# Row norms applied behind the projections instead of ahead of them, in a hybrid encoder layer with experts

## The reference

```python
def rms_norm(x, w):
    y = xf * lax.rsqrt(jnp.mean(xf * xf, axis=-1, keepdims=True) + NORM_EPS)
    return y * w
...
    xn = rms_norm(x, norm1_w)
    proj = xn @ w_in                                   # (tokens, 4096)
    hq, hf_f, hf_b, hi, hg, aq, ak, av = jnp.split(proj, split_points(), axis=-1)
    o_hg = hgrn2_bidirectional(hq, hf_f, hf_b, hi, hg, lb_f, lb_b, hg_norm_w)
    o_da = diff_attention(aq, ak, av, layer, q_norm_w, k_norm_w, lq1, lk1, lq2, lk2, subln_w)
    h = x + (jnp.concatenate([o_hg, o_da], axis=-1) @ w_out)
    return h + expert_choice_moe(rms_norm(h, norm2_w), router_w, w1, w3, w2)
```

## Time and profile before

| | |
|---|---|
| median of 3 runs | 2069.92 us (2067.45 to 2071.37) |
| profiled execution | 2071.38 us, of which the span of the trace is 2069.6 |
| TensorE busy | 2022.5 us, 98% of the span |
| VectorE busy | 1616.7 us, 78% |
| ScalarE busy | 1339.1 us, 65% |
| GpSimd busy | 86.3 us, 4% |
| mean granted TensorE clock | 0.990 |

### The profile page before, as it was taken

The page is one execution under the profiler, slowest core; times in us unless marked ns, Lnnn a source line. Parts: engine busy times, 40 slices in busy tenths (PEclk is TensorE's granted clock), DMA queues, the critical chain, the costliest instruction groups (busy, mean ns, idle before and its releaser), DMA issues.

```text
span 2069.6 us, 27968 instructions
## 1 busy us (share of the span) xinstructions
PE 2022.5 (98%) x10828; PEld 1556.4 (75%) x10828; DVE 1616.7 (78%) x1187; ACT 1339.1 (65%) x1027; POOL 86.3 (4%) x51
## 2 busy tenths in 40 slices
PE   7999999989799999999999999999999999999998
PEld 6899998768677777777777777777777777776776
DVE  4247766764888888888888888888888888888886
ACT  4234433742477777777777777777777777778774
POOL 0000000300000000000000000000000000000000
PEclk9999999989899999999999999999999999999999
DMA  5222224125599999999999999999999999999994
GB/s 162 67 67 74 95 76 160 64 99 195 197 370 365 394 359 390 366 381 377 372 390 363 394 355 392 363 387 373 375 383 362 394 360 399 356 389 369 376 386 152
DMA packets 192388, 618.17 MB, mean 299 GB/s; under 512 B 13680, under 2 KB 38000, under 8 KB 192336
## 3 DMA queue, kind: packets, MB, share of 16 engines
q1 hardware_dynamic: 188640, 604.86, 77.8%
q0 software_dynamic: 3696, 12.59, 2.7%
HBM read 596.96 MB, written 20.45 MB: 298 GB/s over the span
## 4 chain that ended last, share of the span: by engine, by line
PE 95%; DVE 3%; DMA 1%; ACT 1%; issue 0%; POOL 0%; SPq 0%; POOLq 0%; ACTq 0%; DVEq 0%
PE pair L582 29%; PE pair L584 29%; PE pair L583 29%; PE pair L663 2%; PE pair L938 1%; PE pair L736 1%; PE pair L760 1%; PE pair L721 1%; PE pair L884 1%; PE pair L747 0%; DMA x_in<-x 0%; DVE top_tokens L1660 0%; PE pair L703 0%; DMA v_tm<-projected 0%; PE pair L801 0%
## 5 line engine op out<-in xcount | busy, mean ns | idle before, releaser
L1743 DVE TENSOR_TENSOR chunk_low<-ring,chunk_high 128x3072 fp32r<-128x3072 f32 (+1 forms) x384 | 1182.2, 3088 | 221.1 <-ACT chunk_high L1206 221.1
L1206 ACT ACTIVATE chunk_high<-ring 128x3072 fp32r<-128x3072 f32 (+1 forms) x384 | 981.2, 2564 | 212.4 <-PE pair L584 212.1
L582 PE MATMUL pair<-chunk_high,xe_high 128*96 128x512 f32 (+1 forms) x1536 | 579.3, 377 | 1.4 <-DVE xe_low L1737 1.4
L584 PE MATMUL pair<-chunk_high,xe_low 128*96 128x512 f32 (+1 forms) x1536 | 574.8, 374 | 0.0
L583 PE MATMUL pair<-chunk_low,xe_high 128*96 128x512 f32 (+1 forms) x1536 | 573.1, 373 | 0.0
L582 PEld LDWEIGHTS pair<-chunk_high,xe_high 128*96 128x96 f32 x1536 | 248.1, 162 | 90.1 <-DVE chunk_low L1743 2.6
L584 PEld LDWEIGHTS pair<-chunk_high,xe_low 128*96 128x96 f32 x1536 | 247.8, 161 | 90.1
L583 PEld LDWEIGHTS pair<-chunk_low,xe_high 128*96 128x96 f32 x1536 | 248.4, 162 | 87.3
L582 PE MATMUL pair<-chunk_high,hid_high 128*96 128x512 f32 x704 | 280.3, 398 | 0.0
L584 PE MATMUL pair<-chunk_high,hid_low 128*96 128x512 f32 x704 | 276.9, 393 | 0.0
L583 PE MATMUL pair<-chunk_low,hid_high 128*96 128x512 f32 x704 | 276.2, 392 | 0.0
(11 more groups left out here) (209 smaller groups left out, 1855.8 us busy)
## 6 DMA issues: line engine op xcount, KB each, us to landing
ring<-w SPq DMA_DIRECT2D x288, 1536.0 KB, 9.3
ring<-w SPq DMA_DIRECT2D x96, 1024.0 KB, 8.5
raw_w<-w_in SPq DMA_DIRECT2D x16, 1024.0 KB, 5.4
projected<-stage SPq DMA_DIRECT2D x36, 128.0 KB, 1.7
wo_raw<-w_out SPq DMA_DIRECT2D x8, 512.0 KB, 3.4
x_in<-x SPq DMA_DIRECT2D x6, 512.0 KB, 7.8
queries_and_keys<-qk_raw SPq DMA_DIRECT2D x8, 384.0 KB, 2.8
x_again<-x SPq DMA_DIRECT2D x6, 512.0 KB, 4.7
```

The costliest lines, as they stand in the source:

```text
L582: pe.matmul(dst, a_high, b_high, start=first, stop=False)
L584: return pe.matmul(dst, a_low, b_high, start=False, stop=last)
L1206: act.activation(ch[c % SPLIT][:, 0:n], ring[c % RING][:, 0:n], ACT.Copy).then_inc(ch_done, 1)
L1743: dve.tensor_tensor(cl[c % SPLIT][:, 0:n], ring[c % RING][:, 0:n], ch[c % SPLIT][:, 0:n].bitcast(F32), ALU.subtract).then_inc(cl_done, 1)
```

## The change

The transposes take the raw x tiles. The norm's weight, which belongs to the rows of w_in, is multiplied into the weight pieces, and the row scales are applied to the projections: feature-major units by a product of VectorE in PSUM with the scales of all 768 tokens laid out along the free dimension (rstd_bc), token-major units by the scale operand of the evacuation. rstd_bc comes from six products of a matrix of ones with diagonal matrices that hold the row scales. In the pieces of the token-major units the weights are scaled in place, in eight instructions, and then copied in one as before. The numbers of idle products at the start change, and the attention loop gets two idle products at a = 17 to 23.

```diff
-FIRST_FILL = {1: 10, 3: 7}
+FILL_AT = range(SAMPLE_TILES * HEADS + 1, MIX_AT)
+FILL = 2
+FIRST_FILL = {1: 3, 3: 12}
...
-                    sp.dma_start(norm1_bc[:, :], norm1.partition_broadcast(P)).then_inc(norm1_in, 16)
+                    sp.dma_start(norm1_t[:, :], norm1.rearrange("(k p) -> p k", p=P)).then_inc(norm1_in, 16)
...
-            pe.wait_ge(xs_ready, i + 1)
+            pe.wait_ge(x_tile_in[ORDER[i]], 16)
...
+        pe.wait_ge(xl_done, SAMPLE_TILES + 1)
+        pe.wait_ge(ones_set, 1)
+        pe.wait_ge(diag_done, 1)
+        for i in range(TILES):
+            mm = pe.matmul(PC[:, tile(i)], ones[:, :], rstd_diag[:, i, :], start=True, stop=True)
+        mm.then_inc(r_mm, 1)
...
+            if a in FILL_AT:
+                keep_clock(KDEC, FILL)
...
-            act.activation(wh[hc % 2][:, :, :], raw_w[:, :, :], ACT.Copy).then_inc(wh_done, 1)
+            if hc < FM_PIECES:
+                for k in range(KT):
+                    ins = act.activation(wh[hc % 2][:, k, :], raw_w[:, k, :], ACT.Copy, scale=norm1_t[:, k:k + 1])
+                    if hc == 0 and k == KT // 2 - 1:
+                        ins.then_inc(w_half, 1)
+                ins.then_inc(wh_done, 1)
+            else:
+                for k in range(KT):
+                    ins = act.activation(raw_w[:, k, :], raw_w[:, k, :], ACT.Copy, scale=norm1_t[:, k:k + 1])
+                ins.then_inc(w_scaled, 1)
+                act.wait_ge(w_scaled, hc - FM_PIECES + 1)
+                act.activation(wh[hc % 2][:, :, :], raw_w[:, :, :], ACT.Copy).then_inc(wh_done, 1)
...
+        act.wait_ge(x_mean, 1)
+        act.activation(rstd1[:, :], stat1[:, :], ACT.Sqrt).then_inc(x_std, 1)
         high_part(1)
+        act.wait_ge(r_mm, 1)
+        act.activation(rstd_bc[:, :], PC[:, 0:T], ACT.Copy).then_inc(r_done, 1)
...
-                act.activation(qk_raw[q % QK_BUFS][:, n % 3, :], src, ACT.Copy).then_inc(qk_full, 1)
+                act.activation(qk_raw[q % QK_BUFS][:, n % 3, :], src, ACT.Copy, scale=own).then_inc(qk_full, 1)
...
+                    ins = dve.scalar_tensor_tensor(out=wl[hc % 2][:, k, :], in0=raw_w[:, k, :], scalar=norm1_t[:, k:k + 1],
+                                                   in1=wh[hc % 2][:, k, :].bitcast(F32), op0=ALU.mult, op1=ALU.subtract)
...
+            for i in range(TILES):
+                ins = dve.tensor_scalar(rstd_diag[:, i, :], ident[:, :], rstd1[:, i:i + 1], None, ALU.mult)
+            ins.then_inc(diag_done, 1)
...
+            if u == 0:
+                dve.wait_ge(r_done, 1)
+            dve.wait_ge(fm_mm, u + 1)
+            dve.tensor_tensor(pair[u % 2][:, 0:T], pair[u % 2][:, 0:T], rstd_bc[:, :], ALU.mult).then_inc(fm_sc, 1)
             dve.wait_ge(fm_act, u + 1)
```

More of the change, by code:

```diff
@@ L137, in build @@
     stat1 = sb(perm, "stat1", [P, TILES])
+    norm1_t = sb(perm, "norm1_t", [P, KT])
     rstd1 = sb(perm, "rstd1", [P, TILES])
@@ L159, in build @@
     x_in = sb(first, "x_in", [P, TILES, D])
-    x_scaled = sb(first, "x_scaled", [P, TILES, D])
-    norm1_bc = sb(first, "norm1_bc", [P, D])
+    x_squares = sb(first, "x_squares", [P, TILES, D])
+    ones = sb(first, "ones", [P, P])
+    rstd_diag = sb(first, "rstd_diag", [P, TILES, P])
     first.close()
@@ L176, in build @@
     masks_f = sb(before, "masks_f", [P, NL, P])
+    rstd_bc = sb(before, "rstd_bc", [P, T])
     before.close()
@@ L592, in transpose_x @@
             for k in range(KT):
-                mm = pe.transpose(pair[2 + i % 2][:, tile(k)], x_scaled[:, ORDER[i], tile(k)], ident[:, :])
+                mm = pe.transpose(pair[2 + i % 2][:, tile(k)], x_in[:, ORDER[i], tile(k)], ident[:, :])
             mm.then_inc(x_t, 1)
@@ L975, in _ @@
         act.activation(rstd1[:, :], rstd1[:, :], ACT.Sqrt)
-        for g in range(2):
-            squares(2 * g)
-            squares(2 * g + 1)
-            std(g)
-        x_high(0)
-        x_high(1)
+        for i in range(SAMPLE_TILES):
+            x_high(i)
+        act.wait_ge(norm1_in, 16)
         high_part(0)
-        x_high(2)
-        x_high(3)
+        for i in range(SAMPLE_TILES):
+            squares(i)
+        x_high(4)
+        x_high(5)
         squares(4)
         squares(5)
-        std(2)
-        x_high(4)
-        x_high(5)
+        act.wait_ge(x_mean, 1)
+        act.activation(rstd1[:, :], stat1[:, :], ACT.Sqrt).then_inc(x_std, 1)
         high_part(1)
+        act.wait_ge(r_mm, 1)
+        act.activation(rstd_bc[:, :], PC[:, 0:T], ACT.Copy).then_inc(r_done, 1)
         act.wait_ge(setup_v, 5)
@@ L1014, in evacuate_projection @@
             src = PC[:, (n % 2) * 512:(n % 2) * 512 + HC]
+            i = ORDER.index(n % TILES)
+            own = rstd1[:, i:i + 1]
             if n < QK_UNITS:
@@ L1029, in evacuate_projection @@
                 act.activation(stage[m % STAGES][:, :], src,
-                               ACT.Silu if n // TILES in HG_PIECES else ACT.Copy).then_inc(stage_full, 1)
+                               ACT.Silu if n // TILES in HG_PIECES else ACT.Copy, scale=own).then_inc(stage_full, 1)
                 act.wait_ge(stage_full, m + 1)
@@ L1254, in low_part @@
         def low_part(hc):
+            if hc < FM_PIECES:
+                dve.wait_ge(norm1_in, 16)
+                for k in range(KT):
+                    if hc == 0 and k == 0:
+                        dve.wait_ge(w_half, 1)
+                    elif k == (KT // 2 if hc == 0 else 0):
+                        dve.wait_ge(wh_done, hc + 1)
+                    ins = dve.scalar_tensor_tensor(out=wl[hc % 2][:, k, :], in0=raw_w[:, k, :], scalar=norm1_t[:, k:k + 1],
+                                                   in1=wh[hc % 2][:, k, :].bitcast(F32), op0=ALU.mult, op1=ALU.subtract)
+                ins.then_inc(wl_done, 1)
+                return
             dve.wait_ge(wh_done, hc + 1)
@@ L1278, in _ @@
         dve.memset(rstd1[:, :], 1.0).then_inc(table_in, 1)
-        mean_and_rstd(0)
-        dve.wait_ge(norm1_in, 16)
-        scale(0)
-        scale(1)
-        mean_and_rstd(1)
-        scale(2)
-        scale(3)
-        x_low(0)
-        x_low(1)
-        low_part(0)
-        x_low(2)
-        x_low(3)
-        mean_and_rstd(2)
-        scale(4)
-        scale(5)
+        dve.memset(ones[:, :], 1.0).then_inc(ones_set, 1)
+        for i in range(SAMPLE_TILES):
+            x_low(i)
+        low_part(0)
         x_low(4)
         x_low(5)
+        dve.wait_ge(ident_in, 16)
+        row_scales()
         low_part(1)
```

34 lines of the change are left out of this document (16 added, 18 removed).

## The result

The changed kernel takes 2083.38 us, median of 5 runs (2080.21 to 2084.65); the kernel before, beside it, 2069.92 (2067.45 to 2071.84). The ratio is 1.0066, 95% interval 1.0055 to 1.0076, so 13.5 us slower. The forecast was 2076.1 with a range from 2069.0 to 2080.0: the direction was right, the size was too small by half, and the time lies outside the range.

The account below looks back on a forecast made before the run. The first 22.42 us were taken as bound by the chain to the first projection product, later parts by TensorE's waits; 1.9 + 4.0 + 0.3 = 6.2 us on 2071.38 gave 2077.6, less 1.46 for the median 2076.1, range 2069.0 to 2080.0.

Parts of the forecast that it names:

- First product at 19.3: At the start, the first projection product comes at 19.3 instead of 22.42 us, 3.1 us gained.
- The wait before unit 2: TensorE, ready at 40.8, waits 3.8 us for unit 0's banks, freed after the row scales and q_fm.
- unit 2 at 44.6: Unit 2 starts at 44.6 against 42.72, so the gain of 3.1 becomes a loss of 1.9 us.
- the longer slow stretch: At the start, TensorE's longer gap before the first product adds 0.5 us at half clock (0 to 1.4).
- the extra products of the feature-major units: After the start, each extra product of 0.96 us lies under the other unit's 8.3 us and costs nothing.
- The wait at the third token-major unit: TensorE waits about 2 us for ScalarE there, behind the longer scaling and copying of the weight piece.
- From unit 30 each unit is followed by level products and two units last over 8 us, which hides 5.0: Late token-major units: the 5.0 us of scaling and copying each weight piece is hidden and costs nothing.
- a term of 4.0: Token-major weight pieces take 5.0 us for 1.92; waits at units 0, 6, 12, 18 and 24 sum to 4.0 us.
- the idle products: Attention loop: fourteen of 128x128 at 0.11 or 0.22 us each; those of units 19 and 20 cost 0.3 us.
- The rival on them: Idle products keep TensorE's clock up from 419 to 443 us, saving 4.9: 2070.9 us; chance 0.10.
- Half clock in the prompt's units: In the prompt's attention units TensorE still runs at half clock for some 17 us.
- the scaled copy: Weights' high copy: scaled 128x256 copies 0.36 us from start to start, 3.0 for eight; lower bound 0.28, the plain step.

Follow-up runs that it names:

- c_norm_on_x: Changed kernel with the norm's weight multiplied into the transposed x in PSUM by VectorE and all weight pieces copied plain; ratio 1.0019 to the kernel before.
- f_dve_load: Changed kernel with token-major pieces in one scaled pass, plus an unread VectorE product of 128x768 between high copy and low part; ratio 1.0039 to the kernel before.
- the single pass: a_tm_one_pass: changed kernel with token-major weight pieces made by eight scaled high copies and eight scaled low parts, like the feature-major ones; ratio 1.0021 to the kernel before.
- f_act_load: Changed kernel with token-major pieces in one scaled pass, plus an unread ScalarE copy of 128x1536 behind each high copy; ratio 1.0038 to the kernel before.
- the three pairs: Kernels with and without the attention's idle products: changed 1.0066 and 1.0078, before 0.9991 and 1, single pass with early setup 0.9979 and 0.9980.
- f_plain_eight: Changed kernel with token-major pieces in one pass of eight high copies without the scale operand, VectorE's low parts keeping it; ratio 1.0007 to the kernel before.
- a_tm_pool: Changed kernel with GpSimd multiplying the token-major pieces by the norm's weight in place, ScalarE keeping only the plain copy; ratio 1.0062 to the kernel before.
- b_fill: Kernel before with only the fourteen idle products in the attention loop added; ratio 0.9991 to the kernel before.
- a_no_fill: Changed kernel without the idle products in the attention loop; ratio 1.0078 to the kernel before.

## Why the prediction was wrong

**Right.** First product at 19.3, measured 19.07. The wait before unit 2: 3.8 forecast, ended by q_fm, 2.87 measured; unit 2 at 44.6, measured 44.95. Two terms behind it were too small and show only in the shorter wait: TensorE was ready at 42.1 and not at 40.8, because the longer slow stretch cost 1.2 and not 0.5, and the six products with the diagonals took 1.3 and not 0.7. That the extra products of the feature-major units cost nothing behind unit 2: c_norm_on_x has A within 0.3 of before. The wait at the third token-major unit: 2.09 for "about 2".

**Wrong: "From unit 30 each unit is followed by level products and two units last over 8 us, which hides 5.0".** This is the failed step. Here I asked only when ScalarE's own results were due and forgot that VectorE waits for the high copy with merges and key preparations queued behind. Set beside the same products before, TensorE's products come another 1.0 to 1.1 later at each of the four boundaries from unit 30 on (the first level products there: 251.12 against 239.49, 11.6 late, where the group ahead of them was 10.65 late: 245.93 against 235.28), 4.1 in sum where I had 0. The rows at 247.85 show how, and f_dve_load, which adds to VectorE's queue alone, loses 2.85 there against 0.5 in the single pass. The measured time less these 4.1 would have lain inside the range. At the five boundaries before, 4.0 became 6.6 (2.4, 0.7, 1.35, 1.1, 1.0). The size of the block was nearly right (5.1 for 5.0). Taking the scaling out gave 10.6 back in A, against a term of 4.0; f_act_load and f_dve_load show that both queues carry it.

**Missing: the clock behind the new wait.** The text gave the longer slow stretch at the start 0.5 us, but put no price on TensorE restarting behind a wait of 3 to 4. It cost 1.7 us, and it goes with the wait: eight of eight executions with it, none of ten without. The Trainium skill, "TensorE: Matmul & The Clock Gate", section "What's actually happening", says that the throttle is the default and activity releases it. The trace agrees, with the 0.50 at 46 to 48 behind the wait of 2.87.

**Probably wrong sign, small: the idle products.** Forecast +0.3, measured -2.2 in the profiled executions and -1.6 in the mean of B; the ratios of the three pairs give -0.0012, -0.0009 and -0.0001. The rival on them had the mechanism (they keep the clock) with a price of 4.9, three times the -1.6 or more. The 0.11 or 0.22 for each was half of what one takes, since each shows as two records. Half clock in the prompt's units was forecast at some 17 us and was 7. So a part of the distance to the forecast was taken back by what it had with the wrong sign, which is luck.

**Mis-sized: the scaled copy.** 0.36 forecast, 0.40 to 0.41 measured, so 3.3 for eight and not 3.0; the plain step is 0.31, not the 0.28 taken as the bound from below.

The sum, with unit 2's start by the timeline: 2.4 + 1.7 + 10.8 - 2.2 - 0.7 = 12.0, against 1.9 + 4.0 + 0.3 = 6.2 in the forecast. Of the 10.8, 10.6 are the scaling of the pieces. The 5.8 between the two are 0.5 at unit 2, 1.7 for the clock, 2.6 at the five early boundaries, 4.1 at the four late ones and 0.1 elsewhere in A, less 2.5 for the attention and 0.7 behind it. What stays open is why the clock falls behind the wait of 2.09 in three executions and not in the fourth.

## What to carry to other kernels

When an instruction that another engine waits for gets longer, cost it on both queues: behind it on its own, and behind the waiting one on the other. A step repeated at every weight piece uses up the slack of a stage that looks idle on average, and the price then rises steeply: 0.7 us more in ScalarE's block at each of nine pieces cost 1.1 us in A (f_plain_eight to the single pass), and the next 1.9 us, with VectorE's low part starting 1.9 later but 1.0 shorter, cost 9.5. And price a new wait of TensorE with the half clock that can follow it, in a range and not as a sum, because it moves from wait to wait.

## What the runs showed of the hardware

- GpSimd's 128x2048 product of 3.61 us held a VectorE product of 0.25 us for 3.59 (a_tm_pool). A VectorE instruction with one input in SBUF and a constant, 128x12, was held too: 2.48 for 0.16, ending with GpSimd's.
- The half clock is not fixed by the code. b_fill has the code of before up to the attention, but no half clock at the start and unit 2 at 41.02 instead of 42.56; a_no_fill has that of the changed kernel up to the attention, but its slow stretch at unit 2 lasts 6.8 us (43.0 to 49.8) and not 3.4, and it has one more, 3.4 us long at 138.6 to 142.0, with A 2.7 longer. Of the 98 timed executions of the kernel before that stand beside the runs, the 18 with a mean granted clock of 0.994 took 2066.2 us in the mean and the 50 with 0.990 took 2070.6.
- A scale operand read per partition adds 0.09 us to a 128x256 copy of ScalarE (0.31 to 0.40 from start to start).
- The stretch from the last store of moe_rows, ahead of the experts, to the end, identical code, took 1530.1 to 1532.3 us in the profiled executions, so a difference of 2 us in one execution there means nothing. The clock divides them: the seven at 1531.6 to 1532.3 have a slow stretch of 3.4 us some 18 us behind that store, and the eleven at 1530.1 to 1530.7 have not.
